# Gated delta rule inside a two-block transformer kernel: key lengths by one-column products, keys turned once, a convolution piece and three weight conversions moved

## The chip, the cores and the metric

The kernel runs on one NeuronCore of a Trainium2 chip, in one launch. The metric is the time of the program on the device in microseconds (us), as the median of several runs. The engines are TensorE (matmuls, shown as PE, its weight loads as PEld), VectorE (DVE), ScalarE (ACT), GpSimd (POOL) and SyncE (SP), which issues DMAs. The engines run beside each other and meet at semaphores.

## The reference, cut to what matters

Two transformer blocks over 256 tokens of width 1024. The change touches the mixer of one layer, a gated delta rule with 8 heads of 128 channels, which is computed in chunks:

```python
qkv = jax.nn.silu(causal_depthwise_conv((h @ w_in)[..., :3 * W], conv_w))      # four taps
q = l2_normalize(q); k = l2_normalize(k)       # x * rsqrt(sum(x^2) + 1e-6)
g = -exp(a_log) * softplus(a + dt_bias); beta = sigmoid(bt)
diff = g_cum[..., :, None] - g_cum[..., None, :]
decay_incl = jnp.exp(jnp.where(incl, diff, NEG))
lmat = jnp.einsum('bhncd,bhnjd->bhncj', k_beta, k) * decay_strict
sol = lax.linalg.triangular_solve(lmat + eye, rhs, lower=True, unit_diagonal=True)
# then a scan over the chunks carries the state; o is normed, times silu(z), times w_out
```

The mixer's input projection has 32 output tiles of 128 channels: 8 of q, 8 of k, 8 of v and 8 of z.

## The kernel before, in words

All projections are computed with fp32 weights that are split in two: w_hi is the weight rounded to the short matmul type (a cast on ScalarE, L1240, "high part"), w_lo the rest (a subtraction on VectorE, L1838, "low part"). A *unit* is one output tile of 128 channels by 256 tokens: 24 matmuls in three groups of eight (w_hi with in_hi, w_hi with in_lo, w_lo with in_hi). Four slots hold the parts of four units; the high part of unit n + 4 is written when unit n is multiplied, and its low part follows on VectorE in order. SyncE loads the weights in pairs of units; the load of a pair into a raw slot waits for the low parts of the pair that had the slot (lo_done).

In the stage gdn_in, units 0 to 23 give q, k and v. For each, ScalarE copies the result from PSUM to a padded buffer cin[u] and scales it by one tap (L1435, L1436); VectorE adds the other three taps (conv, L2086), then makes a low part. ScalarE applies silu in fours of tiles (L1452). In the kernel before, the loop on VectorE runs conv and low part for all groups: conv(5, u) for u = 0 to 3, each followed by the low part of unit 24 + u.

Units 24 to 31 (z) have nothing to do with the delta rule's matrices. They are put by hand among its steps as z_unit(n) (L821), with the copy z_out(n) and the high part of unit n + 4 on ScalarE. A list written out by hand gives the order of each engine; there is no planner. Each engine works its list in order, and a wait holds up all that is behind it.

The steps of the delta rule, for 16 matrices of 128 x 128 in four groups g of four:

- cols (L808, L809): cumulated decays and betas as columns; ScalarE copies them to gcol (L1468).
- spread_decay (L858): the decays along the rows, in PSUM banks 6, 7, 4, 5. decay_q (L1492) and diff (L2126, VectorE) read them; decay (L1498) applies exp.
- natural_k (L838): the keys are turned (tokens to partitions) into banks 2 and 3; lengths (L1478) squares them with a sum on ScalarE; L1520 to L1522 make the inverse roots of these lengths (gdn_root).
- gram_k (L868): keys times keys. The *triangle* lt (L2143, VectorE) is this times the decay and the scaled inverse length.
- natural_v (L887): the values are turned; scaled_v (L1504) scales them into vb.
- natural_k_again (L848): the keys are turned a second time, into banks 2 to 5; decayed_k (L1511) scales them into kdg.
- gram_q (L879): keys times queries.
- The inversion of the 16x16 corners of the triangle on VectorE, from the transposes of L2153 to those of L2206 (semaphore gdn_scattered). TensorE waits for it before L928, and from there builds the whole inverse, the states and the output. z units 30 and 31 stand among these.

GpSimd multiplies the queries by their decay (L2556) as soon as decay_q is done.

Of the kernel before, what the change touches and what calls it, by code (L numbers as in the profile page):

```python
# [32 lines left out]
ALU = mybir.AluOpType  # L33
# [3 lines left out]
P = 128  # L37
D = 1024
KT = D // P
S = 256  # L40
# [4 lines left out]
EPS = 1e-6  # L45
# [74 lines left out]
def _program(nc, io, ctx):  # L120
# [28 lines left out]
    def sem(name):  # L149
        name = shared.get(name, name)  # L150
        if name not in sems:
            sems[name] = ctx.enter_context(nc.semaphore(name))
        return sems[name]

    def after(name, n):

        return sem(name), n + start.get(name, 0)
# [37 lines left out]
    def area(at, *shape, of=work):  # L195
        v = of[:, at:at + int(np.prod(shape))]
        return v.rearrange("p (a b) -> p a b", a=shape[0]) if len(shape) == 2 else v
# [10 lines left out]
    pair_pt = [area(3072, 2, S), area(3584, 2, S)]  # L208
    bias = [area(4096, 2, S), area(4608, 2, S)]
    ada_rows = [area(4096 + S * n, S) for n in range(2)]  # L210
    cin = [area((S + 3) * u, S + 3) for u in range(GROUP)]
    fbuf = [area(2048 + 512 * u, 2, S) for u in range(2)]
    eb = [area(2048, 4, S), area(1024, 4, S)]
    ml_vnat = area(0, 2, 4 * P)
# [164 lines left out]
    def _(pe):  # L379
# [434 lines left out]
        def z_unit(n):  # L814

            pe.wait_ge(lo_done, LOADED["gdn_in"] + n + 1)
            if n < 30:
                pe.wait_ge(taken, all_taken("gdn_in", max(24, n - 1)))
            for m, (w, a) in enumerate(((w_hi, in_hi), (w_hi, in_lo), (w_lo, in_hi))):
                for k in range(UNIT):  # L820
                    mm = pe.matmul(half(Z_BANK.get(n, n % 2), 0), w[:, n % GROUP, k * P:(k + 1) * P], a[:, k, :],  # L821
                                   start=(m == 0 and k == 0), stop=(m == 2 and k == UNIT - 1))
            mm.then_inc(unit_done, 1)

        def block(t, g, j):
            return proj[:, t + 2 * g + j // 2, (j % 2) * P:(j % 2 + 1) * P]

        SPREAD = (6, 7, 4, 5)

        def natural_k(g):  # L830

            pe.wait_ge(*after("gdn_silu", g // 2 + 1))
            if g < 2:
                pe.wait_ge(taken, all_taken("gdn_in", 23 + g))
            else:
                pe.wait_ge(*after("gdn_length", g - 1))
            for j in range(4):
                mm = pe.transpose(ps[:, 2 + g % 2, j * P:(j + 1) * P], block(8, g, j), ident)  # L838
            mm.then_inc(sem("gdn_natk"), 1)

        def natural_k_again(g):

            if g < 2:
                pe.wait_ge(*after("gdn_length", 3 + g))
            else:
                pe.wait_ge(*after("gdn_vb", 4 * (g + 1)))
            for j in range(4):
                mm = pe.transpose(ps[:, 2 + g, j * P:(j + 1) * P], block(8, g, j), ident)  # L848
            mm.then_inc(sem("gdn_natk"), 1)

        def spread_decay():

            pe.wait_ge(*after("gdn_spread_rows", 4))
            for m in range(2):
                for g in range(4):
                    own = slice(32 * g, 32 * g + 8)
                    t = 34 * g + m
                    mm = pe.matmul(half(SPREAD[g], m), ident[own, t:t + 1].to_broadcast([8, P]), stat[own, 0, :],  # L858
                                   start=True, stop=True)
                    if m:  # L860
                        mm.then_inc(sem("gdn_bc"), 1)

        def gram_k(g):

            pe.wait_ge(*after("gdn_diff", g + 1))
            pe.wait_ge(*after("gdn_qe", g + 1))
            for j in range(4):
                mm = pe.matmul(ps[:, SPREAD[g], j * P:(j + 1) * P], block(8, g, j), block(8, g, j), start=True, stop=True)  # L868
            mm.then_inc(sem("gdn_gk"), 1)
# [12 lines left out]
        def natural_v(g):  # L882

            pe.wait_ge(*after("gdn_silu", 4 + g // 2 + 1))
            pe.wait_ge(*after("gdn_lt", g + 1))
            for j in range(4):
                mm = pe.transpose(ps[:, SPREAD[g], j * P:(j + 1) * P], block(16, g, j), ident)  # L887
            mm.then_inc(sem("gdn_natv"), 1)

        natural_k(0)  # L890
        spread_decay()
        natural_k(1)
        pe.wait_ge(*after("gdn_col_done", 1))
        z_unit(24)
        natural_k(2)
        natural_k(3)
        z_unit(25)
        for g in range(4):
            gram_k(g)
        z_unit(26)  # L900
        for g in range(4):
            natural_v(g)
        z_unit(27)
        for g in range(4):
            natural_k_again(g)
        z_unit(28)
        z_unit(29)
        gram_q(0)
        gram_q(1)

        def quarter(q):
            return slice(32 * q, 32 * q + 32)
# [8 lines left out]
            return [(m, m - 8 * s) for m in range(8 * s, 8 * s + 8)]  # L921

        pe.wait_ge(*after("gdn_kdg", MATS))
        pe.wait_ge(*after("gdn_scattered", 4))
        for s in range(2):
            for m, n in mats(s):
# [294 lines left out]
    def _(act):  # L1221
        act_in = [0]

        def link(ins):

            act_in[0] += 1
            ins.then_inc(sem("act_chain"), 1)
            act.wait_ge(*after("act_chain", act_in[0]))
# [222 lines left out]
        def silu(t):  # L1451
            act.activation(proj[:, t:t + 4, :], proj[:, t:t + 4, :], ACT.Silu).then_inc(sem("gdn_silu"), 1)  # L1452

        for n in range(16, 24):
            act.wait_ge(unit_done, FIRST["gdn_in"] + n + 1)
            evac_conv(n // GROUP, n % GROUP)
            high("gdn_in", n + GROUP)
            if n == 16:
                act.wait_ge(*after("gdn_rows", 2))
                for q in range(4):  # L1460
                    act.copy(stat[32 * q:32 * q + 8, 0, :], rows[0:8, 2, :]).then_inc(sem("gdn_spread_rows"), 1)
            if n in (17, 18):
                act.wait_ge(*after("conv_free", GROUP + 12 + 4 * (n - 17)))
                silu(8 + 4 * (n - 17))
            if n in (19, 20):
                silu(4 * (n - 19))
        act.wait_ge(*after("gdn_cols", 1))
# [2 lines left out]
        def column(n, m):  # L1470

            return kcol[:, n, (m % 2) * 8 + m // 2:(m % 2) * 8 + m // 2 + 1]

        def lengths(g):

            act.wait_ge(*after("gdn_natk", g + 1))
            for j in range(4):
                ins = act.activation(vb[:, 4 * g + j, :], ps[:, 2 + g % 2, j * P:(j + 1) * P], ACT.Square,  # L1478
                                     accum_out=column(1, 4 * g + j))
            ins.then_inc(sem("gdn_length"), 1)  # L1480

        def z_out(n):

# [22 lines left out]

        def decayed_k(g):

            act.wait_ge(*after("gdn_natk", 4 + g + 1))
            for j in range(4):  # L1510
                act.activation(kdg[:, 4 * g + j, :], ps[:, 2 + g, j * P:(j + 1) * P], ACT.Copy,  # L1511
                               scale=column(0, 4 * g + j)).then_inc(sem("gdn_kdg"), 1)

        root_table()
        for g in range(4):
            decay_q(g)
        for g in range(4):
            lengths(g)
        act.wait_ge(*after("gdn_length", 4))
        link(act.activation(kcol[:, 1, :], kcol[:, 1, :], ACT.Ln, bias=eps_col(EPS)))  # L1520
        act.activation(kcol[:, 2, :], kcol[:, 1, :], ACT.Exp, scale=-1.0).then_inc(sem("gdn_root"), 1)
        act.activation(kcol[:, 3, :], kcol[:, 1, :], ACT.Exp, scale=0.5).then_inc(sem("gdn_root"), 1)  # L1522
        for g in range(4):
            decay(g)
        act.wait_ge(*after("gdn_kx", 2))
        act.activation(kcol[:, 0, :], kcol[:, 0, :], ACT.Exp).then_inc(sem("gdn_root"), 1)
        z_out(24)
        for b in range(2):
            act.wait_ge(*after("conv_free", GROUP + 4 * (b + 5)))
            silu(16 + 4 * b)  # L1530
        z_out(25)
        act.wait_ge(*after("gdn_zero", 1))
        act.wait_ge(*after("gdn_lt", 4))
        for b in range(4):
# [1 line left out]
            r = slice(32 * b, 32 * b + 32)  # L1536
            act.activation(ct[r, :, c], lt[r, :, 32 * b + 16:32 * b + 32], ACT.Copy, scale=parity(2)[r, :]
                           ).then_inc(sem("gdn_ct"), 1)
        z_out(26)
        act.wait_ge(*after("gdn_root", 3))  # L1540
        for g in range(4):
            scaled_v(g)
        z_out(27)
        for g in range(4):
            decayed_k(g)
        z_out(28)
        z_out(29)

# [271 lines left out]
    def _(dve):  # L1820
# [282 lines left out]
            ins = dve.tensor_tensor_scan(rows[0:8, 2, c * P:(c + 1) * P], rows[0:8, 4, c * P:(c + 1) * P],  # L2103
                                         rows[0:8, 0, c * P:(c + 1) * P], 0.0, ALU.add, ALU.add)
        ins.then_inc(sem("gdn_rows"), 1)
        project("gdn_in", conv, first_group=1, groups=5)

        def low_half(b):
            return slice(C * b, C * b + 32)
# [19 lines left out]
            ins.then_inc(sem("gdn_diff"), 1)  # L2129

        dve.wait_ge(*after("gdn_col_done", 1))
        for g in range(4):
            diff(g)
        dve.tensor_tensor(kcol[:, 0, 0:8], gcol[:, 32:40], gcol[:, 0:8], ALU.subtract).then_inc(sem("gdn_kx"), 1)
        dve.tensor_copy(kcol[:, 0, 8:16], gcol[:, 8:16]).then_inc(sem("gdn_kx"), 1)
        dve.wait_ge(*after("gdn_root", 1))
        link(dve.tensor_tensor(kcol[:, 2, :], kcol[:, 2, :], gcol[:, 16:32], ALU.mult))
        for g in range(4):
# [4 lines left out]
                ins = dve.scalar_tensor_tensor(lt[:, 4 * g + j, :], ps[:, (6, 7, 4, 5)[g], j * P:(j + 1) * P],  # L2143
                                               kcol[:, 2, at:at + 1], dec[g][:, j, :], ALU.mult, ALU.mult)
            ins.then_inc(sem("gdn_lt"), 1)
        low("gdn_in", 28)
        low("gdn_in", 29)

        dve.wait_ge(*after("gdn_zero", 4))
        dve.wait_ge(*after("gdn_lt", 4))  # L2150
        for b in range(4):
# [572 lines left out]
```

## Time and profile before

| | |
|---|---|
| Median of 3 runs | 861.17 us (860.39 to 863.37) |
| The profiled execution, its own time | 862.46 us |
| Its span from the first to the last instruction | 860.7 us |
| TensorE busy | 829.7 us, 96% of the span |
| VectorE busy | 615.2 us, 71% |
| ScalarE busy | 485.3 us, 56% |
| Mean granted TensorE clock | 0.991 of full speed |

A line of the timeline has the start in us, the time from the first start to the last end in us, the engine, the line of the kernel, the operation, what it writes and reads, and how many instructions are merged in it (x8); in brackets the idle time of the engine before it and what ended that. A 4-byte product takes two matmul instructions, so eight products show as x16. Consecutive matmuls overlap, so the start of the next line says more than the duration.

### The profile page before, as it was taken

How to read it: one execution, taken by the hardware profiler on the slowest of the kernel's cores; microseconds unless marked ns; L12 is line 12 of the kernel's file. 1: busy time of each engine (PE TensorE's matmuls, PEld its weight loads, DVE VectorE, ACT ScalarE, POOL GpSimd, SP SyncE). 2: the span in 40 equal slices, each digit the busy share in tenths (PEclk: the TensorE clock that was granted, in tenths of full speed). 3: DMA queues.
4: the chain of work that ended last, by engine and by line, in shares of the span. 5: the costliest groups of instructions: out<-in, count | busy, mean ns of one | idle time of the engine just before them, and what ended most of it. 6: DMA issues, size and time to landing. Idle time of an engine off the chain costs nothing.

```text
span 860.7 us, 17680 instructions
## 1 busy us (share of the span) xinstructions
PE 829.7 (96%) x6594; PEld 770.8 (90%) x6594; DVE 615.2 (71%) x1054; ACT 485.3 (56%) x898; POOL 63.8 (7%) x70
## 2 busy tenths in 40 slices
PE   6999999999998999999999979999999999999997
PEld 3899988889998998989898859999999999999885
DVE  4487966687899765976867656665678797788543
ACT  3444565476699455584665436656746644555534
POOL 1000001400010002220000022100002020000000
PEclk9999999999999999999999989999999999999999
DMA  9899962804552121533543425444464455455521
GB/s 375 366 369 381 379 241 92 359 23 155 176 185 99 50 100 50 196 133 121 189 161 132 147 86 190 166 145 148 148 221 159 167 174 187 153 188 195 196 98 49
DMA packets 22012, 153.85 MB, mean 179 GB/s; under 512 B 2496, under 2 KB 2752, under 8 KB 3904
## 3 DMA queue, kind: packets, MB, share of 16 engines
q1 hardware_dynamic: 20592, 145.69, 46.4%
q0 software_dynamic: 1360, 7.34, 2.4%
q8 instruction: 41, 0.67, 0.3%
q14 instruction: 19, 0.16, 0.0%
HBM read 151.97 MB, written 1.05 MB: 178 GB/s over the span
## 4 chain that ended last, share of the span: by engine, by line
PE 82%; DVE 7%; ACT 4%; DMA 3%; issue 2%; POOL 0%; DVEq 0%; SPq 0%; ACTq 0%
PE ps L387 40%; PE ps L1200 7%; PE ps L480 6%; PE ps L458 4%; PE ps L421 3%; DVE w_lo L1838 3%; DMA raw<-in_mixed 2%; ACT w_hi L1240 1%; PE ps L430 1%; PE ps L450 1%; PE ps L821 1%; PE ps L631 1%; PE ps L661 1%; PE ps L554 1%; PE ps L577 1%
## 5 line engine op out<-in xcount | busy, mean ns | idle before, releaser
L1838 DVE TENSOR_TENSOR w_lo<-raw,w_hi 128x1024 fp32r<-128x1024 f32 x230 | 284.8, 1244 | 110.8 <-ACT w_hi L1240 110.0
L1240 ACT CAST w_hi<-raw 128x1024 fp32r<-128x1024 f32 (+1 forms) x230 | 239.8, 1050 | 167.9 <-PE ps L387 62.1
L387 PE MATMUL ps<-in_hi,w_hi 128*128 128x256 f32 x1128 | 163.2, 287 | 3.5 <-DVE w_lo L1838 2.2
L387 PE MATMUL ps<-in_lo,w_hi 128*128 128x256 f32 x1128 | 158.3, 283 | 0.0
L387 PE MATMUL ps<-in_hi,w_lo 128*128 128x256 f32 x1128 | 158.3, 283 | 0.0
L387 PEld LDWEIGHTS ps<-in_hi,w_hi 128*128 128x128 f32 x1128 | 146.1, 192 | 9.3 <-DVE w_lo L1838 4.5
L387 PEld LDWEIGHTS ps<-in_hi,w_lo 128*128 128x128 f32 x1128 | 145.5, 192 | 0.0
L387 PEld LDWEIGHTS ps<-in_lo,w_hi 128*128 128x128 f32 x1128 | 145.5, 192 | 0.0
L2086 DVE SCALAR_TENSOR_TENSOR proj<-work,params,proj 128x256 f32 (+1 forms) x72 | 35.5, 493 | 8.0 <-ACT proj L1436 1.8
L1200 PE MATMUL ps<-w_hi,in_lo 128*128 128x512 f32 x88 | 34.2, 389 | 0.0
L1200 PE MATMUL ps<-w_hi,in_hi 128*128 128x512 f32 x88 | 34.2, 389 | 0.0
L1915 DVE SCALAR_TENSOR_TENSOR work<-raw,cs,work 128x1024 f32 x24 | 30.8, 1284 | 4.8 <-DVE w_lo L1838 2.3
L1200 PE MATMUL ps<-w_lo,in_hi 128*128 128x512 f32 x88 | 34.2, 389 | 0.0
L480 PE MATMUL ps<-w_hi,in_hi 128*128 128x512 f32 x80 | 32.5, 407 | 0.0
L480 PE MATMUL ps<-w_hi,in_lo 128*128 128x512 f32 x80 | 31.2, 391 | 0.0
L480 PE MATMUL ps<-w_lo,in_hi 128*128 128x512 f32 x80 | 31.2, 390 | 0.0
L421 PE MATMUL ps<-in_hi,w_hi 128*128 128x256 f32 x108 | 28.0, 297 | 1.4 <-DVE proj L2270 1.0
L421 PE MATMUL ps<-in_hi,w_lo 128*128 128x256 f32 x108 | 27.3, 291 | 0.0
L1734 ACT ACTIVATE proj<-ps,params 128x256 f32<-128x256 f32 x24 | 11.3, 469 | 28.4 <-PE ps L387 28.3
L2474 DVE SCALAR_TENSOR_TENSOR work<-work,params 128x256 f32<-128x256 f32 x44 | 21.3, 484 | 6.4 <-DVE work L2471 1.2
L421 PEld LDWEIGHTS ps<-in_hi,w_hi 128*128 128x128 f32 x108 | 21.7, 201 | 2.2 <-DVE proj L2270 1.4
L421 PEld LDWEIGHTS ps<-in_hi,w_lo 128*128 128x128 f32 x108 | 21.7, 201 | 0.1
(413 smaller groups left out, 1334.9 us busy)
## 6 DMA issues: line engine op xcount, KB each, us to landing
raw<-in_mixed SPq DMA_DIRECT2D x24, 1024.0 KB, 6.6
raw<-in_ffn_up SPq DMA_DIRECT2D x22, 1024.0 KB, 4.7
raw<-in_gdn_in SPq DMA_DIRECT2D x16, 1024.0 KB, 4.8
raw<-in_w_in SPq DMA_DIRECT2D x16, 1024.0 KB, 4.7
raw<-in_merge SPq DMA_DIRECT2D x12, 1024.0 KB, 4.7
raw<-in_ffn_down SPq DMA_DIRECT2D x11, 1024.0 KB, 4.7
raw<-in_branch SPq DMA_DIRECT2D x6, 1024.0 KB, 4.7
raw<-in_moba_out SPq DMA_DIRECT2D x4, 1024.0 KB, 6.3
```

What stands on the lines that cost most here:

```text
L387: mm = pe.matmul(half(u, 0), w[:, u, k * P:(k + 1) * P], a[:, base + k, :], start=(n == 0 and k == 0), stop=(n == 2 and k == UNIT - 1))
L421: pe.matmul(half(u, 0), w[:, u, k * P:(k + 1) * P], in_hi[:, base + k, :], start=(k == 0 and n == 0), stop=False)
L430: mm = pe.matmul(half(u, 0), w_hi[:, u, k * P:(k + 1) * P], in_lo[:, base + k, :], start=False, stop=(k == UNIT - 1))
L458: mm = pe.matmul(out, w[:, u, b * P:(b + 1) * P], a[:, k, :], start=start and n == 0 and m == 0, stop=stop and n == 2 and m == last)
L480: mm = pe.matmul(ps[:, bank + t, :], a[:, base + k, t * P:(t + 1) * P], w[:, k // 2, cols], start=(k == 0 and m == 0), stop=(k == KT - 1 a ...
L1200: mm = pe.matmul(ps[:, 4 + 2 * t + c, :], a[:, k, t * P:(t + 1) * P], w[:, u, cols], start=False, stop=(k == FT - 1 and w is w_lo))
L1240: act.copy(w_hi[:, u, :], src).then_inc(hi_done, 1)
L1734: act.activation(proj[:, n, :], half(n % GROUP, 0), ACT.Identity, bias=param("merge_b", n)).then_inc(taken, 1)
L1838: dve.tensor_tensor(w_lo[:, u, :], src, w_hi[:, u, :].bitcast(F32), ALU.subtract).then_inc(lo_done, 1)
L1915: dve.scalar_tensor_tensor(a, unit_at(r, i, 8), cs[:, bass.ds((i % 2) * GROUP + u, 1)], a, ALU.mult, ALU.add).then_inc(lo_done, 1)
L2086: ins = dve.scalar_tensor_tensor(tile, cin[u][:, tap:tap + S].rearrange("p (a b) -> p a b", a=1), params[:, bass.ds(i * GROUP + (PCOL["gdn ...
L2474: dve.scalar_tensor_tensor(conved, cin[m][:, t:t + S], tap(t), conved, ALU.mult, ALU.add).then_inc(sem("ffn_conv"), 1)
```

## The change

Key lengths are no longer sums on ScalarE over turned keys. ScalarE squares the silued keys as they lie (channels on partitions) into vb, in two instructions inside the unit loop, and TensorE multiplies each 128 x 128 block of squares by a column of ones: 16 one-column products into bank 1. The keys are turned once, and kdg is scaled from these turned keys (banks 2 and 3, each group waits for the scaling of the group two before). The orders of TensorE and ScalarE change with it. On VectorE the last convolution piece, conv(5, 3), and the low part of unit 27 leave the loop; they stand, with the low parts 28 and 29, behind the triangle and ahead of the inversion's transposes. cin[3] moves to another buffer, since the triangle overwrites its old place.

```diff
-    cin = [area((S + 3) * u, S + 3) for u in range(GROUP)]
+    cin = [area((S + 3) * u, S + 3) for u in range(GROUP - 1)] + [area(2560, S + 3, of=core_b)]
 # TensorE
+        def lengths():
+            pe.wait_ge(*after("gdn_ksq", 2))
+            pe.wait_ge(taken, all_taken("gdn_in", 22))
+            for m in range(MATS):
+                at = S + (m % 2) * 8 + m // 2
+                mm = pe.matmul(ps[:, 1, at:at + 1], vb[:, m, :], one, start=True, stop=True)
+            mm.then_inc(sem("gdn_length"), 1)
         def natural_k(g):
...
-                pe.wait_ge(*after("gdn_length", g - 1))
+                pe.wait_ge(*after("gdn_kdg", 4 * (g - 1)))
...
-        def natural_k_again(g):
...
+        spread_decay()
+        lengths()
         natural_k(0)
-        spread_decay()
         natural_k(1)
         pe.wait_ge(*after("gdn_col_done", 1))
         z_unit(24)
         natural_k(2)
+        gram_k(0)
+        gram_k(1)
+        gram_k(2)
         natural_k(3)
+        gram_k(3)
+        pe.wait_ge(*after("gdn_root", 1))
         z_unit(25)
-        for g in range(4):
-            gram_k(g)
         z_unit(26)
-        for g in range(4):
-            natural_v(g)
+        natural_v(0)
+        natural_v(1)
         z_unit(27)
-        for g in range(4):
-            natural_k_again(g)
+        natural_v(2)
+        natural_v(3)
         z_unit(28)
-        z_unit(29)
         gram_q(0)
         gram_q(1)
+        z_unit(29)
...
         pe.wait_ge(*after("gdn_kdg", MATS))
+        pe.wait_ge(*after("gdn_vb", MATS))
         pe.wait_ge(*after("gdn_scattered", 4))
 # ScalarE
                 silu(8 + 4 * (n - 17))
+                act.wait_ge(*after("gdn_silu", n - 16))
+                act.activation(flat(vb[:, 8 * (n - 17):8 * (n - 16), :]), flat(proj[:, 4 * n - 60:4 * n - 56, :]), ACT.Square
+                               ).then_inc(sem("gdn_ksq"), 1)
...
-        for g in range(4):
-            lengths(g)
-        act.wait_ge(*after("gdn_length", 4))
-        link(act.activation(kcol[:, 1, :], kcol[:, 1, :], ACT.Ln, bias=eps_col(EPS)))
+        act.wait_ge(*after("gdn_length", 1))
+        link(act.activation(kcol[:, 1, :], ps[:, 1, S:S + MATS], ACT.Ln, bias=eps_col(EPS)))
...
-        for g in range(4):
-            decay(g)
         act.wait_ge(*after("gdn_kx", 2))
         act.activation(kcol[:, 0, :], kcol[:, 0, :], ACT.Exp).then_inc(sem("gdn_root"), 1)
+        act.wait_ge(*after("gdn_root", 3))
+        decay(0)
+        decayed_k(0)
+        decay(1)
+        decayed_k(1)
+        decay(2)
+        decay(3)
         z_out(24)
+        decayed_k(2)
+        decayed_k(3)
+        z_out(25)
         for b in range(2):
             act.wait_ge(*after("conv_free", GROUP + 4 * (b + 5)))
             silu(16 + 4 * b)
-        z_out(25)
+        scaled_v(0)
+        z_out(26)
+        scaled_v(1)
...
-        z_out(26)
-        act.wait_ge(*after("gdn_root", 3))
-        for g in range(4):
-            scaled_v(g)
+        scaled_v(2)
         z_out(27)
-        for g in range(4):
-            decayed_k(g)
+        scaled_v(3)
         z_out(28)
         z_out(29)
 # VectorE
-        project("gdn_in", conv, first_group=1, groups=5)
+        project("gdn_in", conv, first_group=1, groups=4)
+        for u in range(3):
+            conv(5, u)
+            low("gdn_in", 24 + u)
...
-        low("gdn_in", 28)
-        low("gdn_in", 29)
-
+        conv(5, 3)
+        for n in range(27, 30):
+            low("gdn_in", n)
```

On ScalarE the corner scaling (ct) stands between scaled_v(1) and scaled_v(2). On VectorE the two small kcol instructions move ahead of the differences.

## Rows read from the trace of the kernel before

**Rows 1.** The page: the span, the busy times, the high part of the weights.
```profile
span 860.7 us, 17680 instructions
...
PE 829.7 (96%) x6594; PEld 770.8 (90%) x6594; DVE 615.2 (71%) x1054; ACT 485.3 (56%) x898; POOL 63.8 (7%) x70
...
L1240 ACT CAST w_hi<-raw 128x1024 fp32r<-128x1024 f32 (+1 forms) x230 | 239.8, 1050 | 167.9 <-PE ps L387 62.1
```

**Rows 2.** The chain that ended last, 245 to 335 us: start, us, what.
```profile
269.75 1.09 DVE core_b L2153
...
286.62 2.08 PE ps L928 x64
288.70 3.05 PE ps L821 x24
```

**Rows 3.** TensorE's waits: total us, times, longest.
```profile
PE ps L554 <- DVE work L2416: 3.5, 1, 3.5
PE ps L848 <- ACT core_a L1504: 2.9, 2, 2.5
...
PE ps L421 <- DVE proj L2270: 1.0, 1, 1.0
PE ps L928 <- DVE core_b L2206: 0.8, 1, 0.8
```

**Rows 4.** Timeline of ScalarE in the delta rule's stage.
```profile
239.38 1.06 ACT L1452 ACTIVATE proj<-proj 128x1024 f32<-128x1024 f32 x1
...
247.86 0.38 ACT L1435 COPY work<-ps 128x256 f32<-128x256 f32 x1 [0.78 <-PE ps L387]
...
264.07 1.28 ACT L1452 ACT_TABLE_LOAD   x1
```

**Rows 5.** Timeline of VectorE, the same stretch.
```profile
248.18 1.74 DVE L2086 SCALAR_TENSOR_TENSOR proj<-work,params,proj 128x256 f32 x3
249.84 1.22 DVE L1838 TENSOR_TENSOR w_lo<-raw,w_hi 128x1024 fp32r<-128x1024 f32 x1
...
257.87 4.22 DVE L2126 SCALAR_TENSOR_TENSOR work<-ps,gcol,consts 128x128 f32<-128x128 f32 x16
...
262.35 4.22 DVE L2143 SCALAR_TENSOR_TENSOR work<-ps,kcol,work 128x128 f32<-128x128 f32 x16
```

**Rows 6.** Timeline of TensorE at its one-column products, and the line behind them.
```profile
187.51 1.84 PE L784 MATMUL ps<-small,mem_vnat 128*128 128x1 f32 x16
189.28 3.65 PE L788 MATMUL ps<-work,gdn_wg 128*40 128x256 f32 x16
```

**Rows 7.** Timeline of TensorE, 251 to 279 us.
```profile
251.78 1.15 PE L858 MATMUL ps<-stat,consts 8*128 8x256 f32 x16
252.86 0.66 PE L838 MATMUL ps<-consts,proj 128*128 128x128 f32 x4
253.27 1.20 PE L821 MATMUL ps<-in_hi,w_hi 128*128 128x256 f32 x8
...
256.22 0.61 PE L838 MATMUL ps<-consts,proj 128*128 128x128 f32 x4
...
260.58 3.74 PE L868 MATMUL ps<-proj 128*128 128x128 f32 x32
264.07 1.20 PE L821 MATMUL ps<-in_hi,w_hi 128*128 128x256 f32 x8
...
277.00 2.06 PE L821 MATMUL ps<-in_hi,w_hi 128*128 128x256 f32 x8
```

**Rows 8.** Windows: PE, PEld, DVE, ACT, POOL busy us, granted clock, DMA share, GB/s.
```profile
507.00:508.00 1.00, 0.64 (x6) 0.21 (x4) 0.63 (x2) 0.92 (x3) 0.00 (x0) 0.97 0.57 152
...
514.00:515.00 1.00, 1.00 (x7) 1.00 (x7) 0.99 (x2) 0.00 (x0) 0.89 (x1) 0.62 0.00 0
```

**Rows 9.** Timeline of TensorE around the same stretch.
```profile
504.58 1.99 PE L798 MATMUL ps<-rows,consts 4*128 4x256 f32 x8
506.50 1.14 PE L554 MATMUL ps<-proj 64*128 64x256 f32 x8
511.17 2.08 PE L554 MATMUL ps<-proj 64*128 64x256 f32 x8 [3.54 <-DVE work L2416]
...
514.93 1.12 PE L387 MATMUL ps<-in_lo,w_hi 128*128 128x256 f32 x8
```

More of the change, by code:

```diff
@@ L835, in natural_k @@
             else:
-                pe.wait_ge(*after("gdn_length", g - 1))
+                pe.wait_ge(*after("gdn_kdg", 4 * (g - 1)))
             for j in range(4):
                 mm = pe.transpose(ps[:, 2 + g % 2, j * P:(j + 1) * P], block(8, g, j), ident)
-            mm.then_inc(sem("gdn_natk"), 1)
-        def natural_k_again(g):
[L843 to L848, printed above, removed]
             mm.then_inc(sem("gdn_natk"), 1)
@@ L1472, in column @@
             return kcol[:, n, (m % 2) * 8 + m // 2:(m % 2) * 8 + m // 2 + 1]
[L1474 to L1480, printed above, removed]
         def z_out(n):
@@ L1507, in decayed_k @@
         def decayed_k(g):
-            act.wait_ge(*after("gdn_natk", 4 + g + 1))
+            act.wait_ge(*after("gdn_natk", g + 1))
             for j in range(4):
-                act.activation(kdg[:, 4 * g + j, :], ps[:, 2 + g, j * P:(j + 1) * P], ACT.Copy,
+                act.activation(kdg[:, 4 * g + j, :], ps[:, 2 + g % 2, j * P:(j + 1) * P], ACT.Copy,
                                scale=column(0, 4 * g + j)).then_inc(sem("gdn_kdg"), 1)
@@ L2131, in _ @@
         dve.wait_ge(*after("gdn_col_done", 1))
+        dve.tensor_tensor(kcol[:, 0, 0:8], gcol[:, 32:40], gcol[:, 0:8], ALU.subtract).then_inc(sem("gdn_kx"), 1)
+        dve.tensor_copy(kcol[:, 0, 8:16], gcol[:, 8:16]).then_inc(sem("gdn_kx"), 1)
         for g in range(4):
             diff(g)
-        dve.tensor_tensor(kcol[:, 0, 0:8], gcol[:, 32:40], gcol[:, 0:8], ALU.subtract).then_inc(sem("gdn_kx"), 1)
-        dve.tensor_copy(kcol[:, 0, 8:16], gcol[:, 8:16]).then_inc(sem("gdn_kx"), 1)
         dve.wait_ge(*after("gdn_root", 1))
```

## Prediction

> **What bounds the kernel now.** I read the page first. TensorE is busy for 96% of an 860.7 us span and VectorE for 71% [rows 1], so the whole kernel reads as bound by TensorE; but a share over the span says nothing of the 80 us in which the change lies. The chain of waits between 245 and 335 us answers for them. Up to 269.75 us it passes through ScalarE and TensorE, then it is VectorE alone, from the first 32x32 transpose (L2153) to the last (L2206), and from 286.62 us it is TensorE, one group after the other [rows 2]. I call the VectorE part the inversion. It takes 286.62 - 269.75 = 16.87 us and the change does not touch it. After it TensorE shows no wait until L421 at 330 us. So the end of the kernel moves with one number: when the inversion starts.
>
> The list of TensorE's waits agrees [rows 3]. The largest one of this stage, 2.9 us at the second turning of the keys (L848, behind the scaled values of L1504), is followed by 0.8 us at L928, which waits for the inversion. So the 2.9 us are not worth 2.9 us. Take them away and TensorE comes to L928 earlier, and waits there longer. The most that any rearrangement of TensorE alone can give here is nothing, unless it lets VectorE start the inversion earlier.
>
> **The change, part by part.** All times are on the old time axis; the loop of projections (unit 23, until about 250.6 us) ends as before.
>
> *Squares of the keys.* ScalarE gets two squares of 128x1024 after the key silus. Such an activation takes 1.06 us (L1452, [rows 4]), and each square also waits for the silu's end: some 2.2 us in all. ScalarE waits 0.78 us for TensorE before unit 22 [rows 4] and again before unit 23, so it has caught up by then. One convolution on VectorE is late by an estimated 0.8 us; VectorE handles a unit in 2.79 us (1.66 for the three taps, 248.18 to 249.84, and 1.13 for the low part, recorded as 1.22, whose end overlaps the next start, [rows 5]) and is some 2 us ahead of TensorE's need. Nothing reaches the path.
>
> *Lengths.* Sixteen ScalarE squares with a sum out of PSUM go; sixteen products of one column come, ahead of both turnings of the keys. The trace has the same form at L784: eight products are 16 matmul rows and take 189.28 - 187.51 = 1.77 us [rows 6], as much per product (0.22 us) as the 128-column ones of L868 (32 rows in 3.49 us, 260.58 to 264.07, [rows 7]). So lengths() costs 3.54 us of TensorE, in the open, before z unit 24. The Trainium skill, "TensorE: Matmul & The Clock Gate", section "Wait — 56ns, not 53.3ns?", says that start to start never drops below about 25 ns however small the product is. If that were the price here, 32 rows would be an estimated 0.8 us and not 3.5; the trace of the same form disagrees (110 ns a row), and the page itself says elsewhere that the weight load counts too.
>
> *The order on TensorE, recomputed.* From 251.2 us: spread 1.08 (251.78 to 252.86, [rows 7]), lengths 3.54, two turnings of 0.41 (252.86 to 253.27), z unit 24 2.95 (253.27 to 256.22, [rows 7]), one turning, one gram block of 3.49/4 = 0.87: the first block is there at 260.9 us. VectorE's differences (L2126, 4.22 us) now begin near 254.7 because the last convolution is no longer ahead of them; even if GpSimd's products for the queries, which run beside them, stretch them by a third, an estimate, they are done by 260.5. So the triangle (L2143, 4.22 us recorded, 4.14 until the next can begin, [rows 5]) starts at 261.05, 1.3 us earlier, and ends at 265.2.
>
> *What is moved behind it.* conv(5, 3) at 1.66 us and three low parts of 1.13 us: 5.05 us, so the inversion starts at 270.3 instead of 269.75. Before, only two low parts stood there, with a wait for ScalarE between them. In other words VectorE does the same work ahead of the inversion in both kernels; what it gains by not waiting for the lengths, it loses waiting for the first gram block. **First term: +0.55 us.**
>
> Does something arrive later than 270.3? The last low part (29) needs ScalarE's high part 29, which needs z unit 25. TensorE: three more gram blocks and a turning from 260.9 give 263.9, z 25 ends 266.9, the copy and the cast of 1.05 us [rows 1] are done at 268.3. It is needed at 269.2: 0.9 us to spare. The DMAs whose slots these low parts free bring weights that are first cast after 296 us: hidden.
>
> *The rest of TensorE's work.* z 26 ends at 269.8. The turnings of the values wait for silu(16), which on ScalarE now stands behind high part 29, with a table load of 1.28 us [rows 4] and the silu's 0.96: 270.6. TensorE waits 0.9 us. Then 0.8, z 27, 0.8, z 28, two gram blocks 1.75, z 29: done at 283.0. ScalarE's last scaled value is out before that. The sixteen second turnings that are saved (1.7 us) and the 2.9 us of stall that go both end up here: TensorE stands still from 283.0 to 270.3 + 16.87 = 287.2, for 4.2 us instead of 0.84.
>
> *The clock after that stall.* Before, TensorE stalls for 2.5 us at L848, the granted clock goes to half, and the eight matmuls at 277.00 take 2.06 instead of 1.20 us as at 253.27 [rows 7]; TensorE had 0.84 us to spare, so this cost the kernel little. The nearest row to a stall of 4.2 us is that of 3.54 us at L554: the clock was at half (1.2 GHz) from just before 508 until 514.6 us [rows 8], and 16 products from 511.17 to 514.93 took 3.76 us [rows 9] where at full clock eight of L554 take 1.14 us recorded [rows 9] and eight 256-column products of a unit about a third of its 2.95, near 2.05 together. That is 1.7 us, and here it lies on the path, because L928 and z unit 30 follow the inversion directly. Bounds: 1.0 us (as at 277.00) and 0 if the clock holds. **Second term: +1.7 us.**
>
> *The clock in the lengths.* The trace has one fall that hardly any stall explains: just before 508 us the clock drops to half with only 0.36 us of idle time before it; what ran were 1.95 us of products with 4 rows (L798) and 1.1 us with 64 rows (L554) [rows 8, 9]. So products that use little of the array do not hold the clock, though TensorE counts as busy. The changed kernel has, without a break from 250.6 us, 0.6 us of 8-column transposes, 1.08 us of 8-row products and 3.54 us of one-column products; today the stretch of the first two is cut by turnings and ends at 253.3, and L784's 1.77 us alone brought no fall. I take it that 5.2 us of this do bring one. Its price is not in the trace of this place. From below, it falls at the end of the lengths and costs what the other one costs, 1.7 us; from above, the clock stays at half as long as around 511 us, from 508 to 514.6 (6.8 us with the part before it), all of it in TensorE's stream: 3.4 us. I take the middle. All of it reaches the inversion, for gram block 0 ends later by as much and VectorE has only some 0.5 us of its own ahead of it. **Third term: +2.6 us.** The Trainium skill, the same page, section "HAM oscillation — how this bites in real kernels", puts the rule as avoiding idle gaps of TensorE. By that rule the lengths, without a gap, would cost no clock, and the sum would be by 2.6 us smaller; the fall before 508 us speaks against it as the whole rule, the ones after stalls agree with it.
>
> **Sum.** 0.55 + 1.7 + 2.6 = +4.85 us. The profiled execution took 862.46 us (span 860.7 and 1.8 around it) and would take 867.3; it lay 1.3 us above the median of the runs, 861.17, from which I get 866.0 us. What a measurement can tell from no change is about 0.3%, 2.6 us: below 858.6 or above 863.8.
>
> **Rivals.**
> *A, the clock holds through the lengths.* Only the first two terms stay: +2.25, 863.4 us, with +1.55 to +2.8 by the bounds of the stall's fall. For it: L784 and the products behind it kept their full rate [rows 6], and the weight loads go on at full rate. The page's rule on gaps, named above, says A. Against: the fall before 508 us [rows 8]. It is within 0.3%, but close to its edge.
> *B, the one-column products are cheap.* If their rows follow each other as closely as the 64-column ones of L928, 64 in 2.08 us [rows 2] or 32 ns, the lengths take 1.0 us and gram block 0 is there at 258.4. The floor of the Trainium skill's page, named above, says the same. The sum of VectorE's own work then decides: 254.7 + 4.1 + 0.2 + 4.1 + 5.05 = 268.3, 1.45 us earlier than now, with z 25's high part in time. With full clock 859.7 us, with the stall's fall (-1.45 + 1.7) 861.4. To be faster by over 0.3% the inversion would have to start 2.6 us earlier, before 267.2, and VectorE's own work does not allow that; it would take the loss of a fall of the clock besides, such as the one at L421, whose 1.0 us of stall is in today's chain.
> *C, nothing changes place.* The stall of 4.2 us brings no fall and VectorE is not kept by the gram block: within 0.6 us of before, 861.7. For it: a share of VectorE's time near 255 us is slowed by GpSimd and may not be so after the change.
> *The other side, and from which point:* this kernel forecast is slower; A turns it into no change as soon as the clock costs in the lengths less than 0.4 us, B into no slower at all.
>
> **Chances.** Forecast (fall in the lengths and after the stall) 0.55, A 0.27, B 0.08, C 0.06, something else 0.04. Slower by over 0.3%: 0.51 of the forecast, 0.10 of A and 0.01 of the rest: 0.62. Faster: part of B and of what is not foreseen, 0.08. Same: 0.30. The range from 861.7 (the first term alone) to 868.0 (both falls at their upper bound, 866.8, and 1.2 for the error of the first term) leaves out B's faster half and a longer stretch at half clock.
>
> **What would show it.** Right: L2153's first transpose at 272 to 274 us; half clock in the one-microsecond windows between 253 and 262 us and again around 288 to 291; a wait of TensorE of about 4 us at L928; no wait for scaled values any more. If the clock is full from 250 to 262 us, it is A and L2153 starts near 270.3. If the one-column products take under 2 us, it is B. The forecast goes wrong if the low part 29 waits for its cast (then more than +5), if ScalarE is late in unit 20 to 23 by more than 2 us so that TensorE waits within the loop, or if VectorE's differences last beyond 261 us.

## The result, and the profile after

The changed kernel takes 867.36 us in the median of 4 runs (866.74 to 868.25), the kernel before 861.25 us (860.39 to 863.37). The ratio is 1.0069, with a 95% interval of 1.0054 to 1.0084: about 6 us slower. The span of the profiled execution is 864.8 us against 860.7 [rows 1].

The page after, its span, busy times and clock. TensorE is busy for the same share of the span as before (96%), and its clock is lower in the twelfth and the fourteenth slice (of 21.6 us each), where the changed stage lies.
```profile
span 864.8 us, 17650 instructions
...
PE 833.9 (96%) x6610; PEld 776.4 (90%) x6610; DVE 614.2 (71%) x1054; ACT 483.0 (56%) x868; POOL 62.3 (7%) x70
...
PEclk9999999999989899999999989999999999999999
```

TensorE's waits after, in total us, times, longest. The 2.9 us of L848 [rows 3] are gone, and the wait for the inversion (L932, L928 before) has grown from 0.8 to 3.8 us. The silus of the values are a new wait of 0.9 us.
```profile
PE ps L932 <- DVE core_b L2212: 3.8, 1, 3.8
...
PE ps L421 <- DVE proj L2276: 1.0, 1, 1.0
PE ps L886 <- ACT proj L1456: 0.9, 1, 0.9
```

The timeline of TensorE after. L836 are the one-column products.
```profile
248.96 0.41 PE L808 MATMUL ps<-consts,rows 8*128 8x8 f32 x4
...
250.49 5.06 PE L836 MATMUL ps<-small,core_a 128*128 128x1 f32 x32
255.41 1.95 PE L847 MATMUL ps<-consts,proj 128*128 128x128 f32 x8
257.01 2.06 PE L821 MATMUL ps<-in_hi,w_hi 128*128 128x256 f32 x8
...
288.51 3.68 PE L932 MATMUL ps<-consts,core_b 64*64 64x64 f32 x64 [3.84 <-DVE core_b L2212]
292.12 1.88 PE L821 MATMUL ps<-in_hi,w_hi 128*128 128x256 f32 x8
...
295.82 2.08 PE L943 MATMUL ps<-work,core_b 64*64 64x64 f32 x64
```

The windows after; the number behind POOL's is the granted clock. TensorE has no idle time from 250 to 262 us, and yet its clock falls there.
```profile
250.00:252.00 2.00, 2.00 (x23) 1.67 (x15) 1.93 (x4) 1.98 (x3) 0.00 (x0) 1.00 0.50 111
252.00:254.00 2.00, 2.00 (x14) 2.00 (x14) 1.97 (x9) 1.37 (x5) 1.30 (x2) 0.66 0.98 414
254.00:256.00 2.00, 2.00 (x11) 2.00 (x11) 2.00 (x9) 0.38 (x2) 1.48 (x3) 0.50 0.00 0
256.00:258.00 2.00, 2.00 (x11) 2.00 (x10) 0.96 (x5) 1.97 (x9) 0.00 (x0) 0.50 0.00 0
258.00:260.00 2.00, 2.00 (x13) 2.00 (x13) 0.00 (x0) 2.00 (x8) 0.00 (x0) 0.63 0.00 0
...
286.00:288.00 2.00, 0.00 (x0) 0.00 (x0) 1.94 (x3) 0.00 (x0) 0.00 (x0) 0.69 0.00 0
288.00:290.00 2.00, 1.49 (x28) 1.52 (x30) 1.97 (x3) 0.00 (x0) 0.00 (x0) 0.50 0.00 0
290.00:292.00 2.00, 2.00 (x42) 2.00 (x38) 1.62 (x3) 0.58 (x1) 0.00 (x0) 0.50 0.04 8
```

The timeline of VectorE after: the differences (L2132), the triangle behind a wait of 5.7 us for the first gram block, the moved convolution and three low parts, and the first transposes of the inversion.
```profile
252.65 4.22 DVE L2132 SCALAR_TENSOR_TENSOR work<-ps,gcol,consts 128x128 f32<-128x128 f32 x16
...
262.64 4.23 DVE L2149 SCALAR_TENSOR_TENSOR work<-ps,kcol,work 128x128 f32<-128x128 f32 x16 [5.68 <-PE ps L867]
266.78 1.51 DVE L2089 SCALAR_TENSOR_TENSOR proj<-core_b,params,proj 128x256 f32<-128x256 f32 x3
268.21 3.49 DVE L1841 TENSOR_TENSOR w_lo<-raw,w_hi 128x1024 fp32r<-128x1024 f32 x3
271.62 4.42 DVE L2159 STREAM_TRANSPOSE core_b<-work 32x512 f32<-32x512 f32 x4
```

Two traces don't begin their stage at the same time: the first column transpose (L808) is at 250.63 us before and at 248.96 after, because earlier waits for weights were shorter (the first DMA's by 0.6 us, for instance). So all comparisons below count from L808. The two lines of the kernel before on which this rests:
```profile
250.63 0.41 PE L808 MATMUL ps<-consts,rows 8*128 8x8 f32 x4
...
291.68 2.08 PE L939 MATMUL ps<-work,core_b 64*64 64x64 f32 x64
```
On this axis the inversion starts at 19.12 us before (269.75 - 250.63) and at 22.66 after: 3.54 us later. It takes 16.87 us in one and 16.89 in the other. From L928/L932 to the next group of 64 (L939/L943) there are 5.06 us before and 7.31 after: 2.25 us more. Together 5.8 us, and the span's end is 5.8 us later on this axis (610.1 and 615.8), which is the 6.1 us of the medians within the spread of the runs (1.5 us for the changed kernel).

### The profile page after: what moved, and what is told of

It is laid out like the page before. It is cut to its first block, busy times and chain, and to the rows that moved or that the text cites. A ratio compares the mean times of both kernels' runs of the same rounds, so it can differ in the third digit from the quotient of the medians.

```text
span 864.8 us, 17650 instructions
## 1 busy us (share of the span) xinstructions
PE 833.9 (96%) x6610; PEld 776.4 (90%) x6610; DVE 614.2 (71%) x1054; ACT 483.0 (56%) x868; POOL 62.3 (7%) x70
## 4 chain that ended last, share of the span: by engine, by line
PE 81%; DVE 8%; DMA 5%; ACT 2%; issue 2%; SPq 0%; POOL 0%; DVEq 0%; ACTq 0%
PE ps L387 39%; PE ps L1204 7%; PE ps L480 6%; PE ps L458 4%; PE ps L421 3%; DVE w_lo L1841 3%; DMA raw<-in_mixed 2%; PE ps L430 1%; PE ps L450 1%; PE ps L821 1%; ACT w_hi L1244 1%; DMA raw<-in_moba_first 1%; DMA proj<-in_ada_first 1%; PE ps L554 1%; PE ps L577 1%
## 5 line engine op out<-in xcount | busy, mean ns | idle before, releaser
L2089 DVE SCALAR_TENSOR_TENSOR proj<-work,params,proj 128x256 f32 (+1 forms) x54 | 26.0, 482 | 5.8 <-ACT proj L1440 1.8
L421 PE MATMUL ps<-in_hi,w_hi 128*128 128x256 f32 x108 | 28.0, 298 | 1.4 <-DVE proj L2276 1.0
L421 PE MATMUL ps<-in_hi,w_lo 128*128 128x256 f32 x108 | 27.3, 292 | 0.0
L421 PEld LDWEIGHTS ps<-in_hi,w_hi 128*128 128x128 f32 x108 | 21.8, 201 | 2.2 <-DVE proj L2276 1.4
L421 PEld LDWEIGHTS ps<-in_hi,w_lo 128*128 128x128 f32 x108 | 21.7, 201 | 0.1
```

The source lines that it names most:

```text
L421: pe.matmul(half(u, 0), w[:, u, k * P:(k + 1) * P], in_hi[:, base + k, :], start=(k == 0 and n == 0), stop=False)
L2089: ins = dve.scalar_tensor_tensor(tile, cin[u][:, tap:tap + S].rearrange("p (a b) -> p a b", a=1), params[:, bass.ds(i * GROUP + (PCOL["gdn ...
```

## The experiments

All of them. us are differences from the start of L808 in each trace: triangle is its first instruction, inversion the first transpose, then L928 (L932, L933 or L937 by kernel), the time from it to the next 64x64 group (L939 and so on), and the end of the span. A ratio is to the kernel before in the runs made beside it, estimated from all of these, so it can differ by some 0.0008 from that of the two medians; for a single run it is to the median of the kernel before. The changed kernel was not run again beside the others, so what is said of an experiment against the changed kernel compares two such ratios.

| kernel | ratio, 95% interval | triangle | inversion | L928 | to next group | end |
|---|---|---|---|---|---|---|
| before | 1 | 11.7 | 19.1 | 36.0 | 5.06 | 610.1 |
| changed | 1.0069, 1.0054 to 1.0084 | 13.7 | 22.7 | 39.6 | 7.31 | 615.8 |
| e1_wide | 1.0033, 1.0018 to 1.0047 | 10.5 | 19.5 | 36.4 | 6.58 | 611.1 |
| e2_warm | 1.0036, 1.0020 to 1.0053 | 13.7 | 22.7 | 39.6 | 5.07 | 612.1 |
| e3_both | 1.0018, 0.9999 to 1.0037 | 10.5 | 19.5 | 36.4 | 5.08 | 610.9 |
| e4_in_loop | 1.0048, 1.0030 to 1.0067 | 13.1 | 21.6 | 38.5 | 6.59 | 613.0 |
| e5_better | 1.0003, 0.9987 to 1.0020 | 14.2 | 20.0 | 38.2 | 5.08 | 613.0 |
| e6_mixed | single run, 1.0044 | 11.4 | 21.0 | 37.9 | 6.57 | 613.4 |
| e7_better_warm | 1.0003, 0.9989 to 1.0017 | 13.8 | 20.0 | 38.1 | 5.08 | 610.8 |
| e8_vector_alone | single run, 1.0026 | 11.1 | 20.2 | 37.0 | 6.57 | 612.7 |
| e9_gap | 0.9974, 0.9960 to 0.9989 | 10.6 | 15.9 | 34.1 | 5.08 | 608.7 |
| e10_gap_warm | 0.9979, 0.9967 to 0.9991 | 10.6 | 15.9 | 34.0 | 5.07 | 606.6 |

The last column holds one thing besides: a fall of the clock at L421 that the traces of the kernel before, the changed kernel, e3, e5, e6, e8 and e9 have and those of e1, e2, e4, e7 and e10 don't (see the end). It is worth some 2 us: e9 and e10 agree within 0.1 us up to L932 and end 2.1 us apart.

**e1_wide: the same products, but with columns to stream.**
```diff
-            for m in range(MATS):
-                at = S + (m % 2) * 8 + m // 2
-                mm = pe.matmul(ps[:, 1, at:at + 1], vb[:, m, :], one, start=True, stop=True)
+            for at in range(MATS):
+                m = 2 * (at % 8) + at // 8
+                mm = pe.matmul(ps[:, 1, S + at:S + at + P], vb[:, m, :], ones, start=True, stop=True)
```


> The changed kernel with the 16 length products made 128 columns wide: the moving operand is the full block of ones, the products go in order of their column and each overwrites the surplus of the one before. Rows and weight loads stay as many, only the array has columns to stream. Theory (the one-column products let the clock fall): the granted clock stays at full from 250 to 262 us, the 32 rows take 3.5 us instead of 4.9, and the inversion (first transpose) starts 2.6 to 3.2 us earlier against the end of the unit loop; the kernel is 2.5 to 3.2 us faster than the changed one, near 864.4. Rival (it is the number of products, or their weight loads, that costs): they take as long as before, the clock falls all the same, no change from 867.4.

The timeline and two windows of e1_wide:
```profile
249.03 0.41 PE L808 MATMUL ps<-consts,rows 8*128 8x8 f32 x4
...
250.56 3.84 PE L836 MATMUL ps<-consts,core_a 128*128 128x128 f32 x32
254.23 1.04 PE L847 MATMUL ps<-consts,proj 128*128 128x128 f32 x8
255.03 1.20 PE L821 MATMUL ps<-in_hi,w_hi 128*128 128x256 f32 x8
...
285.44 3.16 PE L932 MATMUL ps<-consts,core_b 64*64 64x64 f32 x64 [3.82 <-DVE core_b L2212]
...
292.02 2.08 PE L943 MATMUL ps<-work,core_b 64*64 64x64 f32 x64
```
```profile
254.00:256.00 2.00, 2.00 (x20) 2.00 (x19) 2.00 (x9) 1.50 (x7) 1.58 (x3) 1.00 0.02 8
256.00:258.00 2.00, 2.00 (x19) 2.00 (x19) 1.04 (x5) 2.00 (x8) 0.00 (x0) 1.00 0.00 0
```
With 128 times the columns the 32 rows take 3.67 us to the next line instead of 4.92, the clock stays at full, and the inversion starts 3.13 us earlier (19.53 against 22.66). In ratio it is 0.36% below the changed kernel, 3.1 us. The intervals don't overlap. The rival, that number or weight loads cost, is out: both are the same here. The fall behind the stall is still there, and it is cheaper than in the changed kernel: 6.58 us to the next group behind a stall of 3.82 us, where the changed kernel has 7.31 behind 3.84.

**e2_warm and e3_both: the stall ahead of L932 filled.**
```diff
         pe.wait_ge(*after("gdn_vb", MATS))
+        keep_warm(8, 2)
         pe.wait_ge(*after("gdn_scattered", 4))
```


> The changed kernel with 8 products of 256 columns, which nobody reads, put into TensorE's stall ahead of L932 (3.4 us of work in a stall of 3.8 us). Theory (the second fall costs on the path): no half clock around 286 to 294 us, L932's 64 rows in 2.1 instead of 3.7 us and z unit 30 in 2.9 instead of 3.6; 2.2 us faster than the changed kernel, near 865.1. Rival (the path behind the stall is held by the other engines, so TensorE's clock is hidden): no change from 867.4, or slower if the products overrun the stall.

The timeline of e2_warm around the inversion's end:
```profile
285.87 3.61 PE L466 MATMUL ps<-consts 128*128 128x256 f32 x16
289.87 2.08 PE L933 MATMUL ps<-consts,core_b 64*64 64x64 f32 x64 [0.38 <-DVE core_b L2213]
291.88 1.22 PE L821 MATMUL ps<-in_hi,w_hi 128*128 128x256 f32 x8
```
L933 takes 2.08 us instead of 3.68 and the stretch to the next group 5.07 instead of 7.31: 2.24 us back from work that nobody reads, while the inversion does not move (22.69). In ratio 0.33%, 2.8 us below the changed kernel, with intervals that just miss each other. The path behind the stall is TensorE's, as the theory has it.

> Both edits together: wide length products and filled stall. Theory: both falls are gone and only the first term of the sum is left, so the kernel is within 0.3 to 0.9 us of the kernel before, 861.2 to 862.2. Rival (a third cost that I have not named): 1.5 us or more stay.

In the trace both effects are gone: inversion at 19.53, to the next group 5.08. What is left there is 0.41 us of a later inversion. The ratios are less tidy: both edits together give back 0.51% (4.4 us), less than the 0.36% and 0.33% of each by itself make together, and the ratio of 1.0018, 1.6 us, has 1 just inside its interval (0.9999 to 1.0037). The trace shows no third cost of 1.5 us, and the interval does not exclude one; this stays open.

**e4_in_loop: VectorE's old order.**
```diff
-        project("gdn_in", conv, first_group=1, groups=4)
-        for u in range(3):
-            conv(5, u)
-            low("gdn_in", 24 + u)
+        project("gdn_in", conv, first_group=1, groups=5)
...
-        conv(5, 3)
-        for n in range(27, 30):
+        for n in range(28, 30):
             low("gdn_in", n)
```


> The changed kernel with VectorE's old order: conv(5, 3) and the low part of unit 27 back in the unit loop, low parts 28 and 29 behind the triangle. Theory (VectorE waits 5.7 us for the first gram block anyway, so the work that was moved is hidden where it was and in the open where it is now): the triangle starts where it did, the inversion starts 0.5 us earlier only, because low part 29 then waits for its high part; 0.5 us faster, near 866.9. Rival (the moved work is the cost of the change): 2.6 us faster, near 864.8.

The timeline of VectorE in e4_in_loop:
```profile
261.85 4.23 DVE L2146 SCALAR_TENSOR_TENSOR work<-ps,kcol,work 128x128 f32<-128x128 f32 x16 [0.33 <-DVE kcol L2140]
265.99 1.21 DVE L1841 TENSOR_TENSOR w_lo<-raw,w_hi 128x1024 fp32r<-128x1024 f32 x1
269.13 1.22 DVE L1841 TENSOR_TENSOR w_lo<-raw,w_hi 128x1024 fp32r<-128x1024 f32 x1 [1.93 <-ACT w_hi L1244]
270.28 4.41 DVE L2155 STREAM_TRANSPOSE core_b<-work 32x512 f32<-32x512 f32 x4
```
From the triangle to the inversion there are 8.43 us instead of 8.98, the 0.55 expected: low part 29 waits 1.9 us for its high part, as said. The triangle itself was 0.54 us earlier: in this execution the lengths' fall lasted 3.4 us (253.5 to 256.9) and not 6.8 (252.6 to 259.5), and a part of that was lost again, because TensorE waited 0.85 us for the scaled keys at the third turning (L847). The ratio is 0.21% lower than the changed kernel's with overlapping intervals; it does not tell 0.5 us from 2.6. The trace does: as long as the lengths keep VectorE waiting, to undo the move gives back 0.55 us. What the move costs without the lengths is e8's question.

**e6_mixed: narrow products one by one among wide ones.** Each of the 16 one-column products stands behind one of the first 16 matmuls of z unit 24.
```diff
+                    if n == 24 and m < 2:
+                        length(8 * m + k)
...
-        natural_k(2)
         gram_k(0)
         gram_k(1)
+        natural_k(2)
         gram_k(2)
```


> The changed kernel with the same 16 one-column products, but each placed behind one of the first 16 matmuls of z unit 24 instead of in a row of their own, and the first two gram blocks ahead of the third turning of the keys. One look, for the trace. Theory (a stretch filled with nothing but narrow products lets the clock fall, not each of them): no half clock from 250 to 262 us, z unit 24 with the 16 products takes 2.95 + 3.5 us, the triangle starts near 10.5 us behind the first column transpose as with wide products. Rival (one-column products are dear or stop the clock wherever they stand): half clock there too, triangle at 13 us or later.

The windows of e6_mixed:
```profile
254.00:256.00 2.00, 2.00 (x20) 2.00 (x19) 2.00 (x9) 0.00 (x0) 2.00 (x3) 1.00 0.24 98
256.00:258.00 2.00, 2.00 (x17) 2.00 (x17) 1.41 (x6) 0.49 (x3) 0.03 (x1) 0.91 0.00 0
258.00:260.00 2.00, 2.00 (x12) 2.00 (x11) 0.17 (x1) 1.97 (x8) 0.00 (x0) 0.50 0.03 8
```
A miss. The unit with its products takes 7.0 us (251.85 to 258.87) instead of 6.5, and the clock falls before 258 us all the same, only later and for a shorter time, so that the triangle starts at 11.4: between the wide form and the row of narrow ones. The first two gram blocks stand 0.4 us earlier here, which also helps it; its later blocks then wait, and the inversion comes at 21.0. So the fall does not need an unbroken row of narrow products. This is one execution, and how few of them would be free was not tried.

**e8_vector_alone: the kernel before with VectorE's part of the change.** The edit is that of e4_in_loop the other way round, with cin[3] in its new place.

> The kernel before with VectorE's part of the change alone: cin[3] in the other buffer, conv(5, 3) and low part 27 behind the triangle. One look, for the trace. Theory: the triangle starts 0.5 to 0.8 us earlier, the inversion 0.8 to 1.5 us later than in the kernel before (19.1 us behind the first column transpose), the later the more the value silus, which now wait for conv(5, 3) ahead of high part 29, hold low part 29. Rival (the work fills a wait of VectorE there): no later than before.

The timeline of TensorE in e8_vector_alone, and a window between its two stalls:
```profile
274.30 0.66 PE L848 MATMUL ps<-consts,proj 128*128 128x128 f32 x4 [2.94 <-ACT core_a L1504]
...
285.68 2.86 PE L928 MATMUL ps<-consts,core_b 64*64 64x64 f32 x64 [2.15 <-DVE core_b L2210]
```
```profile
276.00:278.00 2.00, 2.00 (x19) 2.00 (x19) 1.90 (x6) 2.00 (x8) 0.00 (x0) 1.00 0.04 8
```
The triangle starts 0.6 us earlier than before (11.1), the inversion 1.1 us later (20.2), and behind TensorE's stall of now 2.2 us the clock is at half from 286.7, 1.0 us into L928 (6.57 us to the next group, 1.5 more than before). So this part alone is a loss too, 2.6 us in this trace: it takes the convolution out of a place where VectorE now waits 1.8 us for the first gram block, and puts it on the path. A stall's length alone does not say whether a fall follows: the longer one of 2.94 us at L848 in this same execution brought none, and in the kernel before one of 2.51 us at the same line did.

**e5_better and e7_better_warm: a first try to beat both.** Wide products, VectorE's old order, and low part 29 behind the inversion's first transposes; e7 has 3 products in the stall.

> Wide length products, VectorE's old order (conv(5, 3) and low part 27 in the unit loop), and low part 29 between the inversion's first transposes and the scaling behind them, so that it no longer waits for its high part ahead of them. Theory: VectorE has no wait of over 0.5 us left before the inversion, which starts at 17.1 us behind the first column transpose (kernel before: 19.1, changed kernel: 22.7); the low part then costs its 1.1 us within it, L932 starts near 34.5 (before: 36.0, changed: 39.5), TensorE's stall ahead of it is under 2.5 us and may or may not bring a fall of the clock. 0.1 to 0.2% faster than the kernel before. Rival (the stretch is bound by something that the sum does not name): no better than both fixes of the clock together, 0.1% slower than before.

> The same with 3 products of 256 columns, which nobody reads, in the stall ahead of L932 (1.3 us). Theory: the clock holds at L932 in the profile, 0.2% faster than the kernel before. Rival (the fall does not come at such a stall, or the products overrun it): as without them, or up to 1 us slower.

The timeline of TensorE in e7_better_warm:
```profile
260.20 0.63 PE L847 MATMUL ps<-consts,proj 128*128 128x128 f32 x4 [2.44 <-ACT memkv L1511]
260.67 4.47 PE L867 MATMUL ps<-proj 128*128 128x128 f32 x24
```
A miss of both: inversion at 20.0, not 17.1. With conv(5, 3) ahead of them the differences start at 8.5 us instead of 3.7; ScalarE's decay and the scaled keys wait for them, and TensorE waits 2.4 us at the third turning for its bank. That stall brings a fall of its own, at the gram blocks (24 rows in 4.3 us, 2.7 in e9_gap). No better than before (1.0003 both).

**e9_gap and e10_gap_warm: the work in the gap.** On top of the wide products; the last line of the diff stands behind the inversion's first four transposes.
```diff
         for g in range(4):
             diff(g)
+        conv(5, 3)
+        low("gdn_in", 27)
         dve.wait_ge(*after("gdn_root", 1))
...
-        conv(5, 3)
-        for n in range(27, 30):
-            low("gdn_in", n)
+        low("gdn_in", 28)
...
+        low("gdn_in", 29)
```


> The changed kernel with wide length products; on VectorE conv(5, 3) and low part 27 stand between the differences and the triangle, where it waits for the first gram block, low part 28 stays behind the triangle and low part 29 goes behind the inversion's first transposes. Theory (the change is right in its idea and wrong in its place: there is a gap of 2.7 us ahead of the triangle, the moved work is 2.6 us, and the differences must stay ahead of it or TensorE waits at the third turning as in the run before): triangle at 10.6 us behind the first column transpose, inversion at 16.0 (kernel before: 19.1), L932 at 34.0 (before: 36.0), no half clock before that; 0.2 to 0.3% faster than the kernel before. Rival (as before, something moves in: the value silus or TensorE's z units are later than the inversion): no better than 0.1%.

> The same with 2 products of 256 columns, which nobody reads, ahead of L932 (0.9 us in a stall of 1.5). Theory: if the stall of 1.5 us brings a fall in some executions, this one is up to 1 us faster in the median; if it does not, the same within 0.1%. Rival: the products overrun the stall, slower by up to 0.5 us.

The timeline of VectorE in e9_gap, with no wait between the lines:
```profile
252.84 4.23 DVE L2132 SCALAR_TENSOR_TENSOR work<-ps,gcol,consts 128x128 f32<-128x128 f32 x16
256.98 1.52 DVE L2089 SCALAR_TENSOR_TENSOR proj<-core_b,params,proj 128x256 f32<-128x256 f32 x3
258.42 1.22 DVE L1841 TENSOR_TENSOR w_lo<-raw,w_hi 128x1024 fp32r<-128x1024 f32 x1
259.55 0.17 DVE L2145 TENSOR_TENSOR kcol<-kcol,gcol 128x16 f32<-128x16 f32 x1
259.76 4.23 DVE L2151 SCALAR_TENSOR_TENSOR work<-ps,kcol,work 128x128 f32<-128x128 f32 x16
263.90 1.21 DVE L1841 TENSOR_TENSOR w_lo<-raw,w_hi 128x1024 fp32r<-128x1024 f32 x1
265.03 4.41 DVE L2159 STREAM_TRANSPOSE core_b<-work 32x512 f32<-32x512 f32 x4
```
The inversion starts at 15.9, 3.2 us earlier than in the kernel before; from there to L932 it takes 18.17 us instead of 16.87, most of it for low part 29 (1.1), and L932 comes at 34.1 instead of 36.0. The ratio is 0.9974 (0.9960 to 0.9989), 858.94 us against 860.96: the first version that beats both. The two products of e10 change nothing that can be measured (0.9979): the stall of 1.5 us brought no fall in e9's profile either.

## Why the prediction was right

- **What bounds it: the start of the inversion.** Right. The 2.9 us of TensorE's stall bought nothing; TensorE stood 3.8 us at L932 (4.2 expected), and the inversion began where the sign for it was set, at 273.3 us on the old axis (272 to 274).
- **First term, +0.55 (VectorE's order and the first gram block).** Measured where the clock holds, in e3_both: 19.53 - 19.12 = 0.41 us. The step that was off in it is mostly the stretching of the differences by GpSimd: they took 4.22 us as before, so VectorE waited 2.5 us for the gram block even at full clock (e1_wide and e3_both) and 5.7 us in the changed kernel, where I had given it some 0.5. In e9_gap just this room turned into the gain.
- **Second term, +1.7 (clock after the stall).** The mechanism was right, the size too small for this execution: 2.25 us, because L932 took 3.68 instead of 2.08 us and the unit behind it the rest. I had priced it by a stretch in which half clock lasted 3.4 us into the work (511.17 to 514.6, [rows 8, 9]); here it lasted 5.1 (288.51 to 293.6, from the 0.60 of the window 292 to 294). The size is not fixed: in e1, e4, e6 and e8 the fall at this place cost 1.5 us (6.57 to 6.59 against 5.06), and 1.7 lies between. I gave no upper bound of my own; the range counted 1.7 as one, rival A's "+2.8" would need 2.25, which is worked out nowhere.
- **Third term, +2.6 (clock in the lengths).** Right in mechanism: clock at half from some 252.6 to 259.5 us without an idle gap. Its size is 22.66 - 19.53 = 3.13 us, inside the bounds of 1.7 and 3.4. The 32 rows took 1.4 us more than at L784's rate (4.92 against 3.54), the two turnings 0.8 more (1.60 against 0.82), z unit 24 1.1 more (4.04 against 2.95). That a fall would come at all rested on a single earlier one, just before 508 us, and I gave it little more than even chances; there was luck in being right.
- **The sum** was 4.85, the trace shows 5.8 and the medians 6.1. The three sizes account for it: 0.41 + 3.13 + 2.25 = 5.79, all from traces of one execution each. The first term was too large by 0.1 and the other two too small by 0.5 each, so the sum is not near by errors that cancel. Two slips changed nothing: B's terms add up to 268.15 and not 268.3, and the chain ahead of 269.75 us also holds 1.3 us of VectorE's differences (L2126).
- **Rivals.** A (the clock holds in the lengths) is out by the trace of the changed kernel and by e1_wide. The rule of the Trainium skill, "TensorE: Matmul & The Clock Gate", section "HAM oscillation — how this bites in real kernels", that idle gaps are to be avoided, holds for the fall at L932, and is not the whole rule: the fall in the lengths came with TensorE busy 2.00 of every 2.00 us. One more thing is against it as the whole rule: the stall of 2.94 us in e8 that brought no fall. B (cheap one-column products) is out: the 32 rows took 154 ns each on average, where B had 32. C is out: the stall brought its fall, and VectorE waited 5.7 us for the gram block.
- **What should not be late.** Low part 29 had its margin (high part at 269.9, needed at 270.5), the wait for the value silus was 0.91 us against 0.9 expected, and VectorE was 0.7 us late once in the unit loop against 0.8 expected; TensorE's loop did not notice.

## What to carry to other kernels

Moving sums from ScalarE to one-column products on TensorE costs TensorE as much as full products, and its clock besides: make such products wide, even if all columns but one are thrown away, or keep them few. When a stall of TensorE is taken away, first ask which engine it meets next; here 2.9 us saved became 3.8 us of waiting instead of 0.8 and a clock at half just where the path came back to TensorE. Work that is to leave the path belongs where its engine waits, and not behind the last step that can be named: the same 2.6 us of VectorE were a loss behind the triangle (e8's trace), no gain ahead of the differences (1.0003), and most of a gain of 0.26% between the two.

## What was not expected of the hardware

The stall of 1.0 us at L421 is in every trace, and the same products behind it meet half clock in some and full clock in others. Windows of e1_wide and of e8_vector_alone around it, the granted clock behind POOL's number:
```profile
332.00:335.00 3.00, 3.00 (x28) 3.00 (x27) 3.00 (x8) 3.00 (x11) 1.26 (x2) 1.00 0.00 0
```
```profile
332.00:335.00 3.00, 3.00 (x18) 3.00 (x18) 3.00 (x8) 3.00 (x11) 1.04 (x2) 0.58 0.00 0
```
In the same 3 us 28 matmul rows start in one and 18 in the other. The 2.1 us between the ends of e9 and e10 are of the size by which executions of one kernel spread, so it may be a part of that, and it is a reason why one profile's span should not be compared with another's without looking at every fall. What decides it in an execution was not tried. The second and the third term vary too: the same stall of 3.8 us cost 2.25 us in the changed kernel and 1.5 in e1_wide, and in e4_in_loop the fall of the lengths lasted half as long as in the changed kernel, with the same 16 products.
